# Experts written out instead of looped, router and last expert by halves, idle transposes in the opening: a two-layer encoder trunk on one core

## The chip, the cores and the metric

The kernel runs on 1 core of one Trainium2 chip, in float32 throughout. The metric is the device time of one execution in microseconds. Before the change three runs took 1687.43 to 1688.12 us, median 1687.98 us.

## The reference

Batch 1, 256 positions, width 1024, two layers. Both layers mix tokens in three branches; layer 0 ends with a dense SwiGLU, layer 1 with eight SwiGLU experts of which each token uses two. What matters here:

```python
for i in range(DEPTH):                                # 2 layers
    u = rmsnorm(h, norm_mix[i])
    z = u @ w_in[i]                                   # 1024 x 7620
    ...                                               # three token mixers
    h = h + merged @ w_out[i]
    v = rmsnorm(h, norm_ffn[i])
    if i % 2 == 0: h = h + swiglu(v, dense_wg[j], dense_wu[j], dense_wd[j])
    else:          h = h + moe_swiglu(v, moe_router[j], moe_wg[j], moe_wu[j], moe_wd[j])
    ple_g = sigmoid(rmsnorm(h, norm_ple[i]) @ ple_gate[i])
    h = h + ple_g * (p[i] @ ple_proj[i])
return rmsnorm(h, norm_final)

def moe_swiglu(v, router, wg, wu, wd):
    logits = v @ router
    top_val, top_idx = lax.top_k(logits, 2)
    top_w = softmax(top_val)
    combine = sum(one_hot(top_idx, 8) * top_w[..., None], axis=-2)
    for e in range(8):
        y = y + combine[..., e:e+1] * swiglu(v, wg[e], wu[e], wd[e])   # 1024 x 2816, 2816 x 1024
```

## The kernel before, in words

**Products in three parts.** Each weight is split into a high part (a copy by ScalarE into `whi`, `split_hi`) and a low part (the difference, by VectorE into `wlo`, `split_lo`); so are the activations (`ahi`, `alo`). A product of 128 x 128 by 128 x 512 is three TensorE matmuls (`three`, lines 1366 to 1368). Weights come in granules of 1 MB: two transfers issued by SP, into a ring of 4 slots (`RAW`), of 6 in the experts (`RAW_MOE`). A granule is converted 3 granules before its use (`WR`); SP refills a slot when the low part of its granule has been made (`split`, a wait on `lo_ready`). Each engine's program is written out in its order, and all meet by semaphores.

**Opening.** SP loads the first half of x and the first weights, ScalarE's queue the second half of x and the norm gains. GpSimd writes the identity. TensorE transposes the gains and, when x has landed, x (`transpose_h`, line 1426: 16 transposes of 128 x 128). ScalarE makes the high parts with the gain (line 557), VectorE the low parts (line 881), then both convert the first granules, and the first product starts.

**Router (layer 1).** When half 0 of h is there, TensorE transposes it; behind the last w_out granule, the other half. ScalarE and VectorE copy the transposes out with the gain (lines 716, 1199). 16 router products (line 1715, 32 instructions) follow when all is copied. VectorE finds the two largest logits, their weights, and from three (with the total five) small TensorE products the position of each token in its expert's list of 128 slots. `place_tokens` builds two selection matrices and two combine matrices (lines 1244, 1246). `gather` (lines 1733, 1734) multiplies v, in high and low part, by the selection: 16 instructions in each of two halves. `comb_transposed` turns the combine matrices (line 1739).

**Experts.** All five engines loop four times over two experts; counts of semaphores and the expert's number come from the loop's register. An expert has 33 granules (`ORDER`: two `up` granules for each of 11 slices of 256 channels, one `down` granule each); every granule is 12 matmuls of 512 columns. Behind `down` 2 and 4 stand the two combines of the *previous* expert (line 1747, four instructions each, then VectorE's add to h, line 1065), behind `down` 8 and 9 the gather for the *next* one. In the loop every expert has both: expert 0 combines a zeroed result `Y`, and expert 7 gathers for an expert 8 that selects nothing.

**Behind the experts.** TensorE turns p (line 1653), waits for its low part, does the two combines of expert 7 each followed by VectorE's add, takes a branch (`overflow`, into code for an expert with more than 128 tokens, not entered here), multiplies p by half 0 of ple_proj (12 matmuls), transposes h once VectorE's signal is there (the memset of line 1323, after its own branch), and does the gate products. At the end VectorE adds the gated part tile by tile, ScalarE squares (line 832), GpSimd takes the root (line 471), VectorE norms both tiles (line 866), and SP stores each.

## Time and profile before

| | before |
|---|---|
| median of three runs | 1687.98 us |
| profiled execution | 1688.75 us, of which 1687.0 us span |
| TensorE busy | 1632.1 us, 97% of the span |
| VectorE busy | 1288.3 us, 76% |
| ScalarE busy | 1016.6 us, 60% |
| GpSimd busy | 39.9 us, 2% |
| chain that ended last | 93% TensorE, 3% VectorE, 1% ScalarE, 1% transfers |
| transfers | 411.09 MB, mean 244 GB/s |

The profile shows one execution. The span runs from the first to the last instruction; the execution's own time is 1.75 us longer. A matmul overlaps the next one by its fill and drain, so the step from start to start counts, not the duration shown. Busy time says nothing of the clock: TensorE is as busy at 1.2 GHz as at 2.4 GHz, and "PEclk" in a window is the share of 2.4 GHz that was granted. In a row, "idle before" is how long the engine had stood still, and "<-" who released it.

### The profile page before, as it was taken

The page shows a single profiled execution, that of the slowest core. Times are in us where ns is not written, and L with a number is a line of the kernel's source. Part 1 is how long each engine was busy: PE and PEld are TensorE (multiplying, and loading weights), DVE is VectorE, ACT ScalarE, POOL GpSimd, SP SyncE. Part 2 cuts the span into 40 slices and gives each one's busy share as a digit, 9 for nine tenths or more (in the row PEclk, how much of TensorE's full clock was granted, in tenths as well). Part 3 has the DMA queues.
Part 4 walks back from the last instruction along what each step waited for, and adds up shares of the span by engine and source line. Part 5 has one row for each costly group of instructions (what it writes and reads, how often), then busy time and mean ns, then how long its engine had stood idle before and what let it go on. Part 6 is the DMA issues. An engine that isn't in the chain of part 4 may idle for free.

```text
span 1687.0 us, 22838 instructions
## 1 busy us (share of the span) xinstructions
PE 1632.1 (97%) x7729; PEld 1334.9 (79%) x7729; DVE 1288.3 (76%) x1528; ACT 1016.6 (60%) x1314; POOL 39.9 (2%) x70
## 2 busy tenths in 40 slices
PE   7999999999999999998999989999899998999987
PEld 6887888888888888887788777887788877888765
DVE  4786887545466886885798987989789897898974
ACT  4655434534455655333677776777777776777753
POOL 3100000000001000000000000000000000000000
PEclk9999999999999999997999999999999999999989
DMA  8444445555555454437799998999989999899950
GB/s 273 150 129 153 144 150 181 199 183 196 180 170 169 134 166 150 138 131 234 247 346 329 352 337 300 350 332 350 332 299 355 329 353 330 301 353 331 354 210 25
DMA packets 291217, 411.09 MB, mean 244 GB/s; under 512 B 15842, under 2 KB 221460, under 8 KB 291092
## 3 DMA queue, kind: packets, MB, share of 16 engines
q1 hardware_dynamic: 289296, 407.16, 71.7%
q10 hardware_dynamic: 1796, 2.32, 0.4%
q8 instruction: 71, 1.16, 0.3%
q14 instruction: 54, 0.44, 0.1%
HBM read 408.38 MB, written 1.05 MB: 243 GB/s over the span
## 4 chain that ended last, share of the span: by engine, by line
PE 93%; DVE 3%; issue 1%; DMA 1%; ACT 1%; POOL 0%; ACTq 0%; DVEq 0%; SPq 0%; POOLq 0%
PE ps L1366 27%; PE ps L1368 27%; PE ps L1367 27%; PE ps L1747 2%; PE ps L1591 1%; DVE wlo L849 1%; PE ps L1753 1%; PE ps L1464 1%; PE ps L1734 1%; PE ps L1733 1%; PE ps L1426 1%; PE ps L1474 1%; DMA arena<-in_moe_wu 1%; DVE arena L1122 0%; PE ps L1569 0%
## 5 line engine op out<-in xcount | busy, mean ns | idle before, releaser
L849 DVE TENSOR_TENSOR wlo<-arena,whi 128x1024 fp32r<-128x1024 f32 x774 | 910.9, 1219 | 177.4 <-ACT whi L516 166.2
L516 ACT ACTIVATE whi<-arena 128x1024 fp32r<-128x1024 f32 x774 | 774.1, 1052 | 173.8 <-PE ps L1368 163.9
L1366 PE MATMUL ps<-whi,ahi 128*128 128x512 f32 (+1 forms) x2040 | 824.7, 404 | 20.1 <-DVE wlo L849 18.5
L1368 PE MATMUL ps<-wlo,ahi 128*128 128x512 f32 (+1 forms) x2040 | 799.7, 392 | 0.0
L1367 PE MATMUL ps<-whi,alo 128*128 128x512 f32 (+1 forms) x2040 | 798.8, 392 | 0.0
L1366 PEld LDWEIGHTS ps<-whi,ahi 128*128 128x128 f32 x2040 | 386.0, 189 | 105.0 <-DVE wlo L849 18.7
L1368 PEld LDWEIGHTS ps<-wlo,ahi 128*128 128x128 f32 x2040 | 385.6, 189 | 82.9
L1367 PEld LDWEIGHTS ps<-whi,alo 128*128 128x128 f32 x2040 | 386.6, 190 | 78.5 <-issue 4.6
L849 DVE TENSOR_TENSOR alo<-ps,ahi 128x256 fp32r<-128x256 f32 (+3 forms) x137 | 71.3, 522 | 59.0 <-ACT ahi L516 40.5
L643 ACT ACTIVATE ahi<-ps 128x256 fp32r<-128x256 f32 x88 | 33.8, 384 | 109.4 <-PE ps L1753 109.2
L516 ACT ACTIVATE ahi<-ps 128x512 fp32r<-128x512 f32 (+2 forms) x49 | 29.3, 607 | 65.2 <-PE ps L1681 28.9
L516 ACT ACTIVATE arena<-ps 128x1024 f32<-128x1024 f32 (+2 forms) x41 | 32.7, 808 | 45.7 <-PE ps L1368 16.7
L787 ACT ACTIVATE arena<-ps 128x256 f32<-128x256 f32 x88 | 33.8, 384 | 40.6 <-PE ps L1368 40.6
L683 ACT ACTIVATE arena<-ps,small 128x512 f32<-128x512 f32 x24 | 15.2, 684 | 48.4 <-PE ps L1368 48.4
L1747 PE MATMUL ps<-arena 128*128 128x512 f32 x72 | 37.3, 644 | 5.9 <-DVE alo L849 4.6
L470 POOL TENSOR_SCALAR small<-small 128x2 f32<-128x2 f32 (+1 forms) x11 | 5.3, 485 | 1561.6 <-ACT arena L542 1206.2
L1065 DVE TENSOR_TENSOR h<-h,ps 128x1024 f32<-128x1024 f32 x24 | 29.1, 1213 | 13.2 <-PE ps L1747 7.5
L1279 DVE TENSOR_TENSOR arena<-arena,ps 128x256 f32<-128x256 f32 x88 | 36.4, 413 | 1.1 <-ACT arena L787 1.1
L1734 PE MATMUL ps<-ahi,alo 128*128 128x128 f32 x144 | 36.1, 291 | 0.0
L1733 PE MATMUL ps<-ahi 128*128 128x128 f32 x144 | 35.2, 284 | 0.0
L1753 PEld LDWEIGHTS ps<-ident,arena 128*128 128x128 f32 x176 | 23.9, 139 | 14.0 <-DVE arena L1279 3.6
L1753 PE MATMUL ps<-ident,arena 128*128 128x128 f32 x176 | 33.9, 274 | 0.3
(202 smaller groups left out, 812.8 us busy)
## 6 DMA issues: line engine op xcount, KB each, us to landing
arena<-in_moe_wg SPq DMA_DIRECT2D x176, 512.0 KB, 5.1
arena<-in_moe_wu SPq DMA_DIRECT2D x176, 512.0 KB, 6.7
arena<-in_moe_wd SPq DMA_DIRECT2D x176, 512.0 KB, 6.0
arena<-in_w_in SPq DMA_DIRECT2D x112, 512.0 KB, 4.5
arena<-in_w_branch SPq DMA_DIRECT2D x24, 512.0 KB, 4.6
arena<-in_dense_wg SPq DMA_DIRECT2D x22, 512.0 KB, 4.0
arena<-in_dense_wu SPq DMA_DIRECT2D x22, 512.0 KB, 5.0
arena<-in_dense_wd SPq DMA_DIRECT2D x22, 512.0 KB, 4.3
```

What stands on the lines that cost most here:

```text
L516: return nc.scalar.activation(dst, src, ACT.Copy)
L643: nc.scalar.activation(ahi[:, o:o + 256], bank(4, 256), ACT.Copy).then_inc(m_thi, 1)
L787: nc.scalar.activation(wk(SIL, FS), bank(s % 2, FS), ACT.Silu).then_inc(m_silu, 1)
L849: return V.tensor_tensor(dst, src, hi.bitcast(f32), ALU.subtract)
L1279: V.tensor_tensor(wk(FFN_, FS), wk(SIL, FS), bank(s % 2, FS, FS), ALU.mult)\
L1366: TE.matmul(o, ahi[:, sa], whi[:, sw], start=start, stop=False)
L1367: TE.matmul(o, alo[:, sa], whi[:, sw], start=False, stop=False)
L1368: return TE.matmul(o, ahi[:, sa], wlo[:, sw], start=False, stop=stop)
L1733: TE.matmul(o, ahi[:, vc:vc + P], psel[:, t * P:(t + 1) * P], start=t == 0, stop=False)
L1734: last = TE.matmul(o, alo[:, vc:vc + P], psel[:, t * P:(t + 1) * P], start=False, stop=t == 1)
L1747: last = TE.matmul(bank(6 + half), wk(CSB + q * 256 + t * P, P), wk(Y + half * 512, 512), start=True, stop=True)
L1753: last = TE.transpose(bank(4, P, c * P), wk(FFN_ + c * P, P), ident[:, :])
```

## The change

- *Opening.* SP loads both halves of x ahead of the weights; ScalarE's queue starts with the gains. ScalarE makes one small copy as soon as the identity is there, ahead of its wait for the gains. TensorE runs 16 transposes of the identity before it waits for the gains, and 24 more behind the transposes of x, into a bank that is not read.
- *Router.* The router products are issued by chunks of the width: 0 to 3 behind the last w_out granule, 4 and 5, then 6 and 7, behind the transposes of half 1. ScalarE squares tile 0 of h before it copies chunks 4 and 5 out, and tile 1 after. The total per expert (for the overflow test) goes to a bank and semaphore of its own, and VectorE reads it behind the first conversions of expert 0. The positions are copied in one instruction; the two selection matrices come before the two combine matrices; the gather stands before the transposes of the combine matrices and waits for the first two alone. `up` granule 0 of an expert waits for half 0 of its tokens, granule 1 for half 1.
- *Experts.* All engines have 8 x 33 granules written out, with constants. Expert 0 has no combines and expert 7 no gather. In expert 7, p is turned and split behind `down` 6, where other experts turn the next combine matrices.
- *Last expert.* Its last granule is multiplied by output half; each half is copied out, combined for both tiles and added to h by half. The high and low part of p lie in another place.
- *Final norm.* VectorE multiplies h by the final gain per half, beside the last squares; then VectorE scales tile 0 and ScalarE tile 1 by the root, and each store waits for its tile.

```diff
@@ SP: x, and the experts' weights
-            sp.dma_start(h[:, 0:D], x[0, 0:P, :]).then_inc(x_landed, 16)
+            for t in range(NT):
+                sp.dma_start(h[:, t * D:(t + 1) * D], x[0, t * P:(t + 1) * P, :]).then_inc(x_landed, 16)
...
-            with sp.Fori(0, NE // 2) as it:
-                for m in range(2 * PER_E):
-                    split(M0 + m - RAW_MOE, it)
-                    e = it * 2 + m // PER_E
+            for m in range(N_MOE):
+                split(M0 + m - RAW_MOE)
+                e = m // PER_E
...
@@ ScalarE: opening, router, last copy of an expert, end
-            act.dma_start(h[:, D:2 * D], x[0, P:2 * P, :]).then_inc(x_landed, 16)
...
+                    act.wait_ge(pool_consts, 2)
+                    copy(lbt[:, 12:13], ident[:, 0:1])
                     act.wait_ge(gains_ready, 1)
...
+                    act.wait_ge(h_half, h_ready(1, "out", 1))
+                    square_of(0)
                     for c in range(4, 6):
                         vt_out(c)
-                norm_squares(h_half, h_ready(layer, "out", 1))
+                    square_of(1)
...
+                            if k == PER_E - 1:
+                                act.wait_ge(combined, 2 * e)
+                                if e < NE - 1:
+                                    act.wait_ge(gemm_done, n + 1)
                                     copy(wk(Y, 1024), bank(2, 1024)).then_inc(m_y, 1)
+                                else:
+                                    for half in range(2):
+                                        act.wait_ge(*((down_half, 2) if half == 0 else (gemm_done, n + 1)))
+                                        copy(wk(Y + half * 512, 512), bank(2 + half)).then_inc(m_y, 1)
+                            convert(n + WR)
...
+            act.wait_ge(rstd_ready, 3 * DEPTH + 1)
+            act.wait_ge(u_ready, 4)
+            nc.scalar.activation(u_nat(1), u_nat(1), ACT.Copy, scale=rstd(3 * DEPTH, 1)).then_inc(out_scaled[1], 1)
@@ VectorE: router, last adds, end
-                    V.memset(wk(Y, 1024), 0.0).then_inc(m_y, 1)
...
-                    for t in range(NT):
-                        V.tensor_copy(wk(POS + 16 * t, 8), bank(1, 8, 8 * t))
-                    link(V.reduce_max(wk(GAP + 48, 1), bank(1, 8, 16), AX.X))
-                    V.tensor_copy(biggest[:, :], wk(GAP + 48, 1)).then_inc(pos_ready, 1)
-                    dve.wait_ge(pos_ready, 1)
+                    link(V.tensor_copy(by_tile(POS, 8, 16), bank(1, 16).rearrange("p (t k) -> p t k", k=8)))
...
-                    lo_of_p()
-                    for t in range(NT):
-                        add_combined(t, 2 * NE + t + 1)
-                        dve.wait_ge(comb_added, 2 * NE + t + 1)
+                    for half in range(2):
+                        dve.wait_ge(last_combined, half + 1)
+                        add_to_h(h_half_of(half), bank(6 if half == 0 else 0, 1024).rearrange("p (t f) -> p t f", t=NT))\
+                            .then_inc(comb_added, 1)
+                    dve.wait_ge(comb_added, 2 * NE)
...
+                        dve.wait_ge(gain_row_landed, 32)
+                        dve.wait_ge(h_last, 2 * half + 2)
+                        for t in range(NT):
+                            o = slice(half * 512, half * 512 + 512)
+                            V.tensor_tensor(u_nat(t)[:, o], h[:, t * D + half * 512:t * D + half * 512 + 512], gain_row[:, o],
+                                            ALU.mult).then_inc(u_ready, 1)
...
-            norm(3 * DEPTH, 2)
+            dve.wait_ge(rstd_ready, 3 * DEPTH + 1)
+            V.tensor_scalar(u_nat(0), u_nat(0), rstd(3 * DEPTH, 0), None, ALU.mult).then_inc(out_scaled[0], 1)
@@ TensorE: opening
+            def keep_busy(n):
+                for _ in range(n):
+                    last = TE.transpose(bank(5, P), ident[:, :], ident[:, :])
+                return last
+
             pe.wait_ge(pool_consts, 2)
+            keep_busy(16)
             pe.wait_ge(gains_landed, 64)
...
             for half in range(2):
                 transpose_h("mix", half)
+            keep_busy(24)
@@ TensorE: router and gather
+                    pe.wait_ge(vt_act, 4)
+                    router_products(range(4))
                     pe.wait_ge(h_half, h_ready(1, "out", 1))
                     transpose_h("moe", 1)
                     pe.wait_ge(vt_act, 6)
+                    router_products(range(4, 6))
                     pe.wait_ge(vt_dve, 2)
+                    router_products(range(6, 8)).then_inc(router_done, 1)
...
                     pe.wait_ge(v_lo, NT)
+                    for half in range(2):
+                        gather(half, onehot, 2, gathered)
                     pe.wait_ge(onehot, 4)
                     comb_transposed()
@@ TensorE: experts
+                    for e in range(NE):
+                        q = e % 2
+                        for k, (kind, j, part) in enumerate(ORDER):
+                            n, s = M0 + e * PER_E + k, e * NS + j
+                            if kind == "up":
+                                if k < 2:
+                                    pe.wait_ge(xg_hi, 2 * e + k + 1)
+                                    pe.wait_ge(xg_lo, 2 * e + k + 1)
...
+                            if k == PER_E - 1 and e == NE - 1:
+                                for half, done in ((0, down_half), (1, gemm_done)):
+                                    by_half(n, n % WR, FFT + 256 * (s % 2), half, [bank(2 + half)], False, True, P)\
+                                        .then_inc(done, 1)
...
+                            if j in (2, 4) and e > 0:
...
+                                combine(1 - q, t)
+                            if j == 6:
...
+                                else:
+                                    pe.wait_ge(ct_out, NE)
+                                    turn_p()
+                            if j in (8, 9) and e + 1 < NE:
...
+                                gather(j - 8, onehot, 4 * e + 8, gathered)
+                    pe.wait_ge(comb_added, 2 * NE - 2)
+                    for half in range(2):
+                        pe.wait_ge(m_y, NE + half)
+                        for t in range(NT):
+                            last = TE.matmul(bank((6 if half == 0 else 0) + t), wk(CSB + q * 256 + t * P, P),
+                                             wk(Y + half * 512, 512), start=True, stop=True)
+                        last.then_inc(last_combined, 1)
```

## Rows read from the trace of the kernel before

**Rows 1.** TensorE's waits over the whole span: us in total, times, longest.

```profile
PE ps L1366 <- DVE wlo L849: 18.5, 4, 5.3
```

**Rows 2.** Timeline of the opening: start us, us, engine, line, instruction, [idle before <-releaser].

```profile
7.97 3.44 PE L1426 MATMUL ps<-ident,h 128*128 128x128 f32 x16
...
9.17 1.28 ACT L557 ACT_TABLE_LOAD   x1 [9.17 <-PE ps L1426]
...
14.38 0.71 PE L1366 MATMUL ps<-whi,ahi 128*128 128x512 f32 x1 [2.97 <-DVE wlo L849]
```

**Rows 3.** The chain that ended last: start us, us, what.

```profile
477.44 1.75 PE ps L1426 x16
...
837.62 1.72 PE ps L1747 x4
```

**Rows 4.** Windows in the opening: us, busy by engine, PEclk, DMA share, GB/s.

```profile
14.00:14.50 0.50, 0.12 (x1) 0.15 (x2) 0.50 (x2) 0.50 (x1) 0.00 (x0) 0.94 1.03 377
14.50:15.00 0.50, 0.50 (x2) 0.41 (x3) 0.50 (x1) 0.50 (x2) 0.00 (x0) 0.50 1.08 393
```

**Rows 5.** Timeline of the router passage.

```profile
779.65 1.09 PE L1426 MATMUL ps<-ident,h 128*128 128x128 f32 x8 [1.86 <-DVE h L1065]
...
781.81 6.40 PE L1715 MATMUL ps<-router,arena 128*128 128x8 f32 x32 [1.07 <-ACT arena L716]
...
790.68 2.48 DVE L1231 SCALAR_TENSOR_TENSOR alo<-arena,small,ahi 128x1024 fp32r<-128x1024 f32 x2
...
795.18 0.46 PE L1733 MATMUL ps<-ahi 128*128 128x128 f32 x1
...
803.85 0.79 PE L1366 MATMUL ps<-whi,ahi 128*128 128x512 f32 x1 [1.60 <-DVE alo L849]
```

**Rows 6.** Windows from a combine to the next, across the three boundaries, and their sum.

```profile
938.16:1046.27 108.11, 102.94 (x461) 83.10 (x461) 89.67 (x97) 76.98 (x94) 0.00 (x0) 0.97 0.95 324
...
sum 324.02, PE 308.38 PEld 249.01 DVE 269.07 ACT 230.94 POOL 0.00; mean PE 102.79 PEld 83.00 DVE 89.69 ACT 76.98 POOL 0.00
```

**Rows 7.** The same, the four that lie inside a pass.

```profile
837.62:938.16 100.54, 100.52 (x462) 81.34 (x461) 89.60 (x97) 74.29 (x92) 0.00 (x0) 1.00 1.00 341
...
sum 401.62, PE 401.49 PEld 325.37 DVE 358.42 ACT 297.20 POOL 0.00; mean PE 100.37 PEld 81.34 DVE 89.61 ACT 74.30 POOL 0.00
```

**Rows 8.** Timeline from the last expert to the transposes of h.

```profile
1632.64 0.60 PE L1653 MATMUL ps<-ident,arena 128*128 128x128 f32 x4
...
1637.86 3.78 PE L1747 MATMUL ps<-arena 128*128 128x512 f32 x4 [4.62 <-DVE alo L849]
...
1642.95 3.49 PE L1747 MATMUL ps<-arena 128*128 128x512 f32 x4 [1.31 <-DVE h L1065]
...
1649.00 0.06 DVE L1323 MEMSET arena<- 128x1 f32 x1 [1.23 <-issue]
...
1649.11 1.97 PE L1426 MATMUL ps<-ident,h 128*128 128x128 f32 x16
```

**Rows 9.** Timeline of the end.

```profile
1681.33 2.48 DVE L866 SCALAR_TENSOR_TENSOR arena<-h,small,arena 128x1024 f32<-128x1024 f32 x2 [2.17 <-POOL small L471]
1682.64 1.55 SPq L425 DMA_DIRECT2D out_h<-arena  x2
```

**Rows 10.** Timeline of half a gather: its first product and the first behind it.

```profile
902.64 0.22 PE L1733 MATMUL ps<-ahi 128*128 128x128 f32 x1
...
904.37 0.44 PE L1366 MATMUL ps<-whi,ahi 128*128 128x512 f32 x1
```

**Rows 11.** Groups by shape: scaling by a value per row on VectorE.

```profile
L910 DVE TENSOR_SCALAR arena<-arena,small 128x256 f32<-128x256 f32 x2 | 0.7, 354 | 4.7 <-ACT arena L612 4.7
...
L910 DVE TENSOR_SCALAR arena<-arena,small 128x128 f32<-128x128 f32 x2 | 0.6, 288 | 0.6 <-ACT arena L610 0.5
```

**Rows 12.** Windows of 10 us inside the first pass of the expert loop.

```profile
830.00:840.00 10.00, 10.00 (x43) 7.56 (x42) 9.91 (x15) 7.80 (x10) 0.00 (x0) 1.00 1.06 363
...
980.00:990.00 10.00, 10.00 (x47) 8.24 (x46) 9.33 (x10) 7.69 (x10) 0.00 (x0) 1.00 0.75 279
```

More of the change, by code:

```diff
@@ L311, in build @@
         XG, FFT = 2048, 4096
+        PT = (4096, XG)
         def blocks(ap, m):
@@ L859, in convert @@
                     split_lo(n % WR, raw_of(n), width_of(n), lambda i: dve.wait_ge(hi_ready, 2 * n + i + 1))
-            def norm(r, done):
-                dve.wait_ge(rstd_ready, r + 1)
-                dve.wait_ge(gain_row_landed, 16 * done)
-                for t in range(NT):
-                    V.scalar_tensor_tensor(out=u_nat(t), in0=h[:, t * D:(t + 1) * D], scalar=rstd(r, t),
-                                           in1=gain_row, op0=ALU.mult, op1=ALU.mult).then_inc(u_ready, 1)
             split = [0]
@@ L1401, in wide_granule, with by_half @@
                 ins.then_inc(gemm_done, 1)
-            def by_half(n, ring, a_base, half, outs, first, last):
+            def by_half(n, ring, a_base, half, outs, first, last, a_pitch=SEQ):
                 for c in range(2):
@@ L1407, in by_half @@
                     for t, o in enumerate(outs):
-                        ins = three(o, a_base + c * SEQ + t * P, ring * GRAN + c * D + half * 512, 512,
+                        ins = three(o, a_base + c * a_pitch + t * P, ring * GRAN + c * D + half * 512, 512,
                                     first and c == 0, last and c == 1)
@@ L1707, in _, with router_products @@
                 else:
+                    pe.wait_ge(router_landed, 16)
+                    def router_products(chunks):
+                        for c in chunks:
+                            for t in range(NT):
+                                last = TE.matmul(bank(2 + t, NE), wk(VT + c * SEQ + t * P, P),
+                                                 router[:, c * NE:(c + 1) * NE], start=c == 0, stop=c == KC - 1)
+                        return last
+                    pe.wait_ge(vt_act, 4)
+                    router_products(range(4))
                     pe.wait_ge(h_half, h_ready(1, "out", 1))
@@ L1710, in _ @@
                     pe.wait_ge(vt_act, 6)
+                    router_products(range(4, 6))
                     pe.wait_ge(vt_dve, 2)
-                    pe.wait_ge(router_landed, 16)
-                    for t in range(NT):
-                        for c in range(KC):
-                            last = TE.matmul(bank(2 + t, NE), wk(VT + c * SEQ + t * P, P),
-                                             router[:, c * NE:(c + 1) * NE], start=c == 0, stop=c == KC - 1)
-                    last.then_inc(router_done, 1)
+                    router_products(range(6, 8)).then_inc(router_done, 1)
                     pe.wait_ge(sel_ready, 1)
@@ L1721, in _ @@
                     TE.matmul(bank(1, NE, 8), ones[:, :], s0, start=True, stop=False)
[L1722 to L1724 removed]
+                    TE.matmul(bank(1, NE, 8), later[:, :], s1, start=False, stop=True).then_inc(pos_done, 1)
+                    TE.matmul(bank(4, NE), ones[:, :], s0, start=True, stop=False)
+                    TE.matmul(bank(4, NE), ones[:, :], s1, start=False, stop=True).then_inc(total_done, 1)
                     def gather(half, ready, onehot_value, done):
@@ L1850, in _ @@
                 pe.wait_ge(pt_lo, layer + 1)
-                by_half(first, first % WR, 4096, 0, [bank(PROJ[0] + t) for t in range(NT)], True, True)
+                by_half(first, first % WR, PT[layer], 0, [bank(PROJ[0] + t) for t in range(NT)], True, True)
                 for half in range(2):
@@ L1854, in _ @@
                     transpose_h("ple", half)
-                by_half(first, first % WR, 4096, 1, [bank(PROJ[1] + t) for t in range(NT)], True, True).then_inc(gemm_done, 1)
+                by_half(first, first % WR, PT[layer], 1, [bank(PROJ[1] + t) for t in range(NT)], True, True).then_inc(gemm_done, 1)
                 for i, (half, q) in enumerate(PLE_ORDER[1:]):
```

225 lines of the change are left out of this document (100 added, 125 removed).

## The prediction

> **What bounds the kernel now.** I read first the share of busy time: TensorE 97%. The chain of waits that ended last is 93% TensorE, so a change pays where TensorE stands still, works at its lower clock, or does work that nobody needs. The list of waits names the first kind [rows 1]: 18.5 us before products that wait for VectorE's low parts, in four waits: the opening and three loop boundaries. The timeline of the opening shows 16 transposes over 3.44 us, 215 ns each [rows 2]; 16 of them take 1.75 us at the full clock [rows 3]. So the opening ones ran at 1.2 GHz. The clock record first drops to half at 14.4 us [rows 4]; a clock that drops had been full, so it rose behind those transposes and was lost in the 3 us of idleness before the first product at 14.38. The router passage is a chain of small steps with TensorE at half clock [rows 5]. The experts are a loop of four passes with two experts each; cut at the same combine product in every expert, the time from one to the next is 108.0 us across a boundary [rows 6] and 100.4 us inside a pass [rows 7]. The last stretch is serial again: combines, adds and transposes one after the other [rows 8], then root, norm and stores [rows 9].
>
> **The sum, part by part** (against the profiled execution, 1687.0 us of span, 1688.75 us in all; the median of the runs shown is 0.77 us below that).
>
> *Opening.* SP takes the second half of x, the gains start one issue (0.4 us) sooner, ScalarE loads its table before it is needed, and TensorE runs 16 idle transposes before the gains and 24 behind the transposes of x. The table load stands in the chain now: 1.28 us between the transposes and the first high part [rows 2]. With it gone and the gains sooner the first low weights are ready at 14.38 - 1.28 - 0.45 = 12.6 us, at most 0.3 us sooner still. TensorE starts no earlier than the 24 transposes allow: x's transposes end near 11.0; if the clock rises there, as it did before, 24 x 0.109 = 2.6 us put the first product at 13.6. That is 0.8 us, and the eight products that ran 427 ns apart instead of 227 give 1.7 (the cold stretch was 14.38 to 17.87). Together 2.5; I take 2.6 as the 16 earlier ones may raise the clock already (then 3.8). If the idle transposes do not hold the clock, 24 x 0.215 = 5.2 us end at 16.2 and the opening loses 1.8. Bounds -1.8 and 3.8; the drop at 14.4 is the row nearest to this case, and it speaks for holding.
> The Trainium skill (ScalarE: Activation LUTs, What ACT_TABLE_LOAD costs) gives a switch of tables 1283 ns and a drain of some 1380 ns more. The trace has the first, and the next instruction 20 ns behind it, so the drain isn't there; by the page the low weights would be ready 1.4 us earlier still, which the 24 transposes would swallow.
>
> *Router.* Four of the eight pairs of router products move into TensorE's wait for the second half of h. Before, all 32 instructions took 6.40 us from 781.81 at mostly half clock [rows 5]. Now 16 run in the gap from 777.6 (ending near 779.4), 8 behind the fifth and sixth chunk, 8 behind VectorE's two. ScalarE squares tile 0 before those chunks, which puts them at 781.8 instead of 781.2, and its second square ends a little sooner. Router end: 781.85 + 0.8 + 1.6 = 784.3 instead of 788.2. VectorE's chain is the same 2.4 us up to the low parts of v, about 0.3 us longer since the two sigmoids now queue behind ScalarE's high parts: low parts from 787.05, 2.48 us, then one copy and two selections (0.75) instead of two copies, a maximum, a cast and four selections: gather at 790.35, against 795.18. After the gather TensorE waited 1.6 us for the high and low part of the second half; now expert 0 asks only for the first half, which was ready during the second gather, and the two combine transposes (0.45) stand there instead: 1.2 more. Sum 6.0, with the gathers and the first products still at half clock. Bounds 4.0 and 9.5 (clock full, below). The moved maximum and the four later operations on VectorE lie beside the products of expert 0.
>
> *Expert 0's empty combine.* Before, expert 0 added a zeroed result: two combines of 1.72 us each [rows 3]; 3.5 with the slower product behind them. VectorE's two adds and two memsets go with them, hidden.
>
> *Loop boundaries.* The three intervals with a boundary make 324.02 us [rows 6], the four without 401.62 [rows 7], 100.4 each: 324.0 - 3 x 100.4 = 22.8 us. Each is some 5.1 us of idleness (the register and branch work of ScalarE, VectorE and TensorE one after the other, then low parts) and then 12 products at 427 instead of 227 ns. Written out, the step from expert 1 to 2 is the step from 0 to 1, which shows no wait. Bounds 21 and 23.5: inside a pass an expert is 0.7 us longer than its products, transposes, combines and gathers add up to, so there is little more in constants instead of registers.
>
> *Last expert.* The gather for an expert that doesn't exist goes: two halves of 1.73 us [rows 10]; four transposes of p come where two combine transposes were (+0.3). 3.2.
>
> *From the experts to the gate.* T is the end of the last expert's products, 1632.64 now [rows 8]. Today p is turned behind T, its high and low parts queue behind conversions, and the two combines start at 1637.86, at half clock, each followed by VectorE's add: 3.78 and 3.49 us. The transposes of h start at 1649.11 = T + 16.5. In the new order half 0 of the result is complete 1.4 us before T and ScalarE copies it (0.6) before T; the four combine products run from T at full clock (2 x 1.72 = 3.44), the add of half 0 beside half 1. Then TensorE does the first 12 products of p (2.72): T + 6.2. VectorE: T + 3.5, add 1.22, 1.23 us of branch work before its signal (as the idle time before the memset shows): T + 6.05. So the transposes start at T + 6.2: 10.3 us. If TensorE's own branch shows, 1.2 less; bounds 8.5 and 10.6. What is late next is the branch on VectorE, level with the products of p.
>
> *The end.* The last norm was 2 x 1.24 us on VectorE behind the root, the stores behind each [rows 9]. Now the gain is multiplied in by VectorE while the last square and the root run (2 x 0.69 from 1679.2, done before 1681.25), and the two tiles are scaled side by side: ScalarE 1.05, VectorE from its rows of 128 and 256 elements, 288 and 354 ns [rows 11], an estimated 288 + 7 x 66 = 750 ns. The second store can go at 1682.5 instead of 1683.8, but the two transfers then overlap more. I take 0.9, bounds 0.3 and 1.3.
>
> Sum: 2.6 + 6.0 + 3.5 + 22.8 + 3.2 + 10.3 + 0.9 = 49.3 us. 1688.75 - 49.3 = 1639.45 for the profiled execution, 0.77 less for the median: 1638.7 us.
>
> **Rivals.** (a) *The stream of weights becomes the bound.* The experts read 528 transfers of 524,288 bytes, 276.8 MB, now in 829 us from their first product; without the boundaries, the combine and the gather it is 799 us, 346 GB/s. For: the transfer share stands near 1.0 in most windows, and a boundary is a rest for the stream. Against: ScalarE never waits for a transfer inside the experts, windows reach 363 GB/s, and late in a pass (980 to 990) the stream idles a quarter of the time because the ring is full [rows 12]. If some 333 GB/s were the most, experts would take as long as before and 29.5 us would be lost: 1668 us. Chance 0.05. The Trainium skill (DMA: Bandwidth & Descriptors, the table of limits at its head) gives about 358 GB/s of HBM per core; by that, as an estimate, the experts need 773 us at least, under my 799, but expert 0 alone (97 us, 357 GB/s) stands at the edge, and would be the place where it first shows.
> (b) *Only the expert part pays.* The idle transposes run at half clock and delay the opening by 1.8, the router chain gives 3 as another small step is late, the tail gives 6 and the stores nothing: 29.5 - 1.8 + 3 + 6 = 36.7, 1651 us. For: these parts hang on semaphores in a row, where one overlooked step takes a microsecond each. Against: each term above is half removed work. Chance 0.08.
> (c) *The clock stays full through the router*, as TensorE now has work where it idled from 777.6 to 779.6: 32 gather products 0.104 us shorter and 12 to 14 of the first expert products 0.2 us shorter give 6 us more, 1632.6 us. Against: the 6.4 us of router products, busy throughout, did not hold it before. Chance 0.08.
> (d) *Slower than before*: the written-out instructions of four engines come late, because they share the transfer engines with weights at 350 GB/s. It decides from 49.3 us over the 264 granules of the experts, 0.19 us per granule; at 0.25 it would be 1704 us. Against: one pass is already 200 us without a jump, and TensorE shows no such wait there. Chance 0.02.
>
> **How the numbers follow.** Forecast 0.77, (a) 0.05, (b) 0.08, (c) 0.08, (d) 0.02. The lower bounds of all terms add up to 38.3 us (1649.7), the upper ones to 55.9 (1632.1); all at one end is unlikely, so 1632 to 1647 holds the forecast and (c), and most of what lies short of (b). 0.2% is 3.4 us, about what a measurement of this kernel can tell from no change: faster 0.97, same 0.01, slower 0.02.
>
> **What would show it.** The intervals between the same combine product in successive experts: all near 100.4 us, the first shorter by 3.5, none of 108. First product near 13.6 us, 227 ns to the next. Gather near 795.2 - 2.6 - 4.8 = 787.8 and expert 0 from 795.3. h transposed 6.2 us behind the last expert product. Wrong would be: ScalarE waiting for transfers inside the experts (a), the idle transposes 215 ns apart to their end (b), gathers 109 ns apart (c), or new waits on no semaphore in the experts (d).

## The result and the profile after

The changed kernel takes 1640.55 us (median of four runs, 1639.43 to 1640.70), the kernel before in the same comparison 1687.70 us (1686.59 to 1688.12): ratio 0.972, 95% interval 0.9703 to 0.9737. The forecast was 1638.7 us. Profiled against profiled it is 1688.75 to 1640.61 us, 48.1 us less, where the sum had 49.3. Below, each stretch is read at one instruction that both kernels have; the column "earlier" is how much sooner it starts, counted from the start of the span, and "this stretch" is what the stretch itself gave.

| at | before | after | earlier | this stretch | forecast |
|---|---|---|---|---|---|
| end of the opening, ninth product of 512 columns | 17.87 | 15.07 | 2.80 | 2.8 | 2.6 |
| expert 0, transposes behind slice 1 | 814.89 | 804.94 | 9.95 | 7.2 | 6.0 |
| expert 0, its slice 9 | 900.97 | 887.29 | 13.68 | 3.7 | 3.5 |
| first instruction behind the last expert's products (T) | 1632.64 | 1593.29 | 39.35 | 23.4 loops, 2.3 last expert | 22.8, 3.2 |
| transposes of h behind the experts | 1649.11 | 1601.04 | 48.07 | 8.7 | 10.3 |
| end of the span | 1687.0 | 1638.9 | 48.1 | 0.0 | 0.9 |

The page of the changed kernel: shares of busy time, and the transfers in 40 slices (GB/s).

```profile
PE 1615.3 (99%) x7727; PEld 1327.3 (81%) x7727; DVE 1284.1 (78%) x1520; ACT 1007.3 (61%) x1307; POOL 38.8 (2%) x70
...
GB/s 284 152 129 154 155 129 188 194 195 181 190 187 179 132 145 149 144 145 190 226 365 351 363 352 335 350 333 362 352 335 351 328 364 345 339 354 330 353 291 26
```

Full slices of the experts now move 328 to 365 GB/s, and ScalarE waits for no transfer there: rival (a) is refuted. Four slices lie above the 358 GB/s of that rival's estimate (365, 363, 362 and 364). TensorE's list of waits, changed kernel (us in total, times, longest), answers to [rows 1]; of the 18.5 us none is left:

```profile
PE ps L1744 <- DVE arena L1227: 2.1, 1, 2.1
PE ps L1435 <- DVE arena L1328: 1.4, 1, 1.4
PE ps L1757 <- DVE ahi L1245: 1.4, 1, 1.4
...
PE ps L1378 <- issue: 1.0, 1, 1.0
```

The first row is the router's small products, which waited 2.1 us before the change too; the third is the router's wait for the selection matrices. The second and the fourth are new: 1.4 us before the transposes of h and 1.0 before a product of the last expert.

*Opening*, timeline of the changed kernel, for [rows 2]:

```profile
2.15 3.67 PE L1624 MATMUL ps<-ident 128*128 128x128 f32 x16 [2.15 <-POOL ident L444]
...
2.78 1.28 ACT L517 ACT_TABLE_LOAD   x1 [2.78 <-issue]
...
7.19 3.57 PE L1435 MATMUL ps<-ident,h 128*128 128x128 f32 x16
...
10.60 2.79 PE L1624 MATMUL ps<-ident 128*128 128x128 f32 x24
...
13.13 0.48 PE L1378 MATMUL ps<-whi,ahi 128*128 128x512 f32 x1
...
13.45 0.40 PE L1379 MATMUL ps<-whi,alo 128*128 128x512 f32 x1
```

The 24 transposes take 2.79 us, the full clock, and the product behind is followed after 0.32 and then 0.24 us. Half clock would put 0.43 between them.

*Router*, the same timeline, for [rows 5]:

```profile
774.87 1.84 PE L1730 MATMUL ps<-router,arena 128*128 128x8 f32 x16
...
778.25 3.37 PE L1730 MATMUL ps<-router,arena 128*128 128x8 f32 x16 [0.61 <-ACT arena L721]
...
784.10 2.48 DVE L1236 SCALAR_TENSOR_TENSOR alo<-arena,small,ahi 128x1024 fp32r<-128x1024 f32 x2
...
787.46 0.44 PE L1757 MATMUL ps<-ahi 128*128 128x128 f32 x1 [1.41 <-DVE ahi L1245]
...
794.31 0.65 PE L1763 MATMUL ps<-ident,arena 128*128 128x128 f32 x2
```

The first 16 router instructions take 1.84 us, 115 ns each, at the full clock. The second 16 start behind 0.61 us of idleness and take 3.37: the granted clock falls from 1.00 to 0.50 at 778.5, 0.3 us into them. The gather runs at half clock.

*Experts*, windows from a combine to the next, for [rows 6, 7]: no interval is longer than another.

```profile
924.34:1024.65 100.31, 100.27 (x462) 81.43 (x461) 89.64 (x97) 74.29 (x92) 0.00 (x0) 1.00 1.01 346
...
1425.82:1526.08 100.26, 100.22 (x462) 81.43 (x461) 89.14 (x94) 74.29 (x92) 0.00 (x0) 1.00 1.01 347
sum 601.74, PE 601.52 PEld 488.58 DVE 537.37 ACT 445.75 POOL 0.00; mean PE 100.25 PEld 81.43 DVE 89.56 ACT 74.29 POOL 0.00
```

*Last expert to the transposes of h*, timeline, for [rows 8]:

```profile
1587.69 2.36 DVE L863 TENSOR_TENSOR wlo<-arena,whi 128x1024 fp32r<-128x1024 f32 x2
...
1588.50 0.38 ACT L647 ACTIVATE ahi<-ps 128x256 fp32r<-128x256 f32 x1
...
1589.97 0.42 DVE L863 TENSOR_TENSOR alo<-ps,ahi 128x256 fp32r<-128x256 f32 x1
1590.49 0.47 PE L1378 MATMUL ps<-whi,ahi 128*128 128x512 f32 x1 [0.97 <-issue]
...
1593.29 3.59 PE L1841 MATMUL ps<-arena 128*128 128x512 f32 x8
...
1593.98 2.00 ACT L517 ACTIVATE whi<-arena 128x1024 fp32r<-128x1024 f32 x2
1595.06 2.36 DVE L863 TENSOR_TENSOR wlo<-arena,whi 128x1024 fp32r<-128x1024 f32 x2 [1.99 <-ACT whi L517]
1597.34 2.35 DVE L1071 TENSOR_TENSOR h<-h,ps 128x1024 f32<-128x1024 f32 x2
1600.93 0.06 DVE L1328 MEMSET arena<- 128x1 f32 x1 [1.24 <-issue]
1601.04 1.97 PE L1435 MATMUL ps<-ident,h 128*128 128x128 f32 x16 [1.43 <-DVE arena L1328]
```

VectorE's queue is the story, twice. The high part of the last slice's transposes is ready at 1588.88, but VectorE is in a conversion until 1590.05, makes the low part by 1590.39, and the product starts 0.10 us behind it (1590.49). The profile names no releaser for that stall of 0.97 us; the product starts 0.10 us behind the same low part in three kernels below, too. Then VectorE waits 1.99 us for a high part, makes a low part that nobody needs yet (2.36), and then comes to the two adds (2.35), its branch (1.24) and the signal.

*End*, timeline, for [rows 9]:

```profile
1631.20 1.29 DVE L1363 TENSOR_TENSOR arena<-h,arena 128x512 f32<-128x512 f32 x2
...
1631.93 0.62 POOL L479 TENSOR_TENSOR small<-small 128x2 f32<-128x2 f32 x1 [24.03 <-ACT arena L843]
...
1633.65 1.15 ACT L848 ACTIVATE arena<-arena,small 128x1024 f32<-128x1024 f32 x1 [1.79 <-POOL small L472]
1633.72 0.75 DVE L1367 TENSOR_SCALAR arena<-arena,small 128x1024 f32<-128x1024 f32 x1 [1.22 <-POOL small L472]
1634.50 0.83 SPq L426 DMA_DIRECT2D out_h<-arena  x2
```

### The profile page after: what moved, and what is told of

Its sections match the earlier page's. It is cut to its first block, busy times and chain, and to the rows that moved or that the text cites. A ratio compares the mean times of both kernels' runs of the same rounds, so it can differ in the third digit from the quotient of the medians.

```text
span 1638.9 us, 20095 instructions
## 1 busy us (share of the span) xinstructions
PE 1615.3 (99%) x7727; PEld 1327.3 (81%) x7727; DVE 1284.1 (78%) x1520; ACT 1007.3 (61%) x1307; POOL 38.8 (2%) x70
## 4 chain that ended last, share of the span: by engine, by line
PE 95%; DVE 3%; issue 1%; ACT 0%; DMA 0%; POOL 0%; ACTq 0%; POOLq 0%; DVEq 0%
PE ps L1378 28%; PE ps L1380 28%; PE ps L1379 27%; PE ps L1600 2%; PE ps L1771 1%; PE ps L1777 1%; PE ps L1473 1%; PE ps L1758 1%; PE ps L1435 1%; PE ps L1757 1%; DVE wlo L863 1%; PE ps L1483 1%; DVE arena L1128 0%; PE ps L1578 0%; DVE arena L1123 0%
## 5 line engine op out<-in xcount | busy, mean ns | idle before, releaser
L679 ACT ACTIVATE arena<-ps,small 128x512 f32<-128x512 f32 (+1 forms) x16 | 10.9, 682 | 37.8 <-PE ps L1380 37.8
L1757 PE MATMUL ps<-ahi 128*128 128x128 f32 x128 | 31.7, 286 | 1.4 <-DVE ahi L1245 1.4
L1758 PE MATMUL ps<-ahi,alo 128*128 128x128 f32 x128 | 32.4, 293 | 0.0
L1186 DVE SCALAR_TENSOR_TENSOR arena<-ps,small,arena 128x256 f32<-128x256 f32 x22 | 9.6, 480 | 28.4 <-ACT arena L751 28.4
```

Of the source, the lines that this page charges most:

```text
L1757: TE.matmul(o, ahi[:, vc:vc + P], psel[:, t * P:(t + 1) * P], start=t == 0, stop=False)
L1758: last = TE.matmul(o, alo[:, vc:vc + P], psel[:, t * P:(t + 1) * P], start=False, stop=t == 1)
```

## The experiments

Kernels that ran together share a chip and its runs of the kernel before: medians 1686.7 us for the loop experiments, 1686.65 for the next four, 1686.57 for the last four. The medians of the kernel before differ by up to 1.4 us from comparison to comparison and its single executions by up to 9 (1682.2 to 1691.3), so ratios are compared, and where they can't decide, rows.

### Loops: which engine's jump costs what

All four change the kernel before. First, every loop of the experts is written out, with nothing else of the change:

```diff
-                    with <engine>.Fori(0, NE // 2) as it:
+                    for it in range(NE // 2):
```

> The kernel before with nothing changed but the expert loops of all engines, written out (empty combine and empty gather stay). Both theories: the three boundaries and only they go, 3 x 7.6 to 7.8 = 23 us (1664.7 us), all intervals between combines near 100.3 us. If the written-out code cost something elsewhere (instructions that come late), less than 20 us.

1662.77 us (1662.30 to 1662.99), ratio 0.9862 (0.9846 to 0.9879): 24 us less. The window across its first boundary is like one of the changed kernel:

```profile
936.88:1037.22 100.34, 100.30 (x462) 81.44 (x461) 89.63 (x97) 74.30 (x92) 0.00 (x0) 1.00 1.01 345
```

So the loops alone are worth 24 us, half of the change, and the other parts together the other half. Next, the same edit in TensorE's program only:

> Only TensorE's expert loop is written out; SP, ScalarE and VectorE still loop. Theory A (TensorE's own jump is the 5.1 us; the others run three granules ahead and hide theirs): nearly all of the 23 us go, 1665 to 1668 us. Theory B (the prediction's: the jumps of ScalarE, VectorE and TensorE one after the other, then low parts): TensorE still waits at each boundary, 3 x 2 us and more remain, 1671 us or above.

1676.79 us (1672.72 to 1680.17), ratio 0.9936 (0.9918 to 0.9954): 10 us less. The three intervals with a boundary fall from 108.0 us to between 104.26 and 104.62, not to 100.3. Its waits of TensorE, and a timeline of its first boundary:

```profile
PE ps L1753 <- DVE arena L1279: 7.1, 3, 2.7
```

```profile
1012.41 1.28 ACT L516 ACT_TABLE_LOAD   x1
1015.73 1.28 ACT L787 ACT_TABLE_LOAD   x1
1017.57 2.36 DVE L849 TENSOR_TENSOR wlo<-arena,whi 128x1024 fp32r<-128x1024 f32 x2 [3.73 <-issue]
...
1020.31 0.69 PE L1753 MATMUL ps<-ident,arena 128*128 128x128 f32 x2 [2.72 <-DVE arena L1279]
```

TensorE runs on into the next expert and meets VectorE, which lost 3.73 us in its own jump; ScalarE's loop has two table loads in each pass, eight in all; with ScalarE written out there is one in the whole expert part. Then the reverse, SP, ScalarE and VectorE written out and TensorE in its loop:

> The reverse: SP, ScalarE and VectorE written out, TensorE still loops. Theory A: no gain, 1686 to 1688 us, intervals of 108 us stay. Theory B: one to three us per boundary go, 1679 to 1685 us.

1682.31 us (1678.00 to 1684.81), ratio 0.9973 (0.9961 to 0.9985): 4.4 us less, the intervals 104.73, 106.99 and 107.79. TensorE's jump alone costs 4.4 to 7.5 us per boundary with its slow products. Its idleness there is 2.56, 3.71 and 4.54 us; why it differs from boundary to boundary is open. 10 and 4.4 do not add up to 24: each jump hides part of the other's. Either time alone lies where the prediction's serial account put it; the two together contradict it. Removing one jump uncovers the other, which is why the prediction, which priced the boundary as a whole, came out and a price per engine would not have. Last, TensorE in its loop is given work to the very end of each pass:

```diff
+                        pe.wait_ge(ct_out, it * 2 + 3)
+                        for _ in range(32):
+                            TE.transpose(bank(5, P), ident[:, :], ident[:, :])
```

> The kernel before with 32 transposes of the identity at the end of each of the four passes of TensorE's loop, 3.5 us of work at full clock in the 5.1 us of idleness. If the second part of a boundary's price is the clock, the 12 products behind it run 227 instead of 427 ns apart and an interval falls from 108.0 to 105.6 us, 3 x 2.4 = 7 us in all (1680.5 us), the last pass adding up to 1 us. If the jump waits until the transposes are done, the idleness comes behind them and the interval grows by up to 3.5 us instead.

1693.91 us, ratio 1.0046 (1.003 to 1.0062): 7 us slower, intervals 111.1 us. Timeline of its first boundary:

```profile
1006.54 3.65 PE L1806 MATMUL ps<-ident 128*128 128x128 f32 x32
1014.80 0.79 PE L1366 MATMUL ps<-whi,ahi 128*128 128x512 f32 x1 [4.61 <-issue]
1015.39 0.63 PE L1367 MATMUL ps<-whi,alo 128*128 128x512 f32 x1
```

The 4.61 us stand behind the transposes, released by nothing that the profile shows (4.62 and 4.52 at the other two boundaries, against 5.09 to 5.30 without the transposes). So 3.65 us of filler hide 0.5 to 0.8 us: the jump hardly runs beside work that is still queued, and the clock is lost in it all the same: 0.59 and 0.43 us from product to product.

### Opening: what holds the clock

The experiments from here on change the changed kernel. Both groups of idle transposes go:

```diff
-            keep_busy(16)
...
-            keep_busy(24)
```

> The changed kernel without the 16 and the 24 idle transposes of the opening; the early table load and the order of loads stay. If the clock is what the idle transposes buy: first product at 12.3 us instead of 13.1, but the first 8 to 12 products 427 ns apart; the opening is 0.8 us quicker to its first product and 1.7 to 2.5 us slower after it, in all about 1.3 us slower than the changed kernel (1641.9 us). If they bought nothing, 0.9 us faster.

1639.09 us (1638.13 to 1640.43), ratio 0.972 (0.9703 to 0.9737), the ratio of the changed kernel. The half clock isn't there: the first product starts sooner than in the changed kernel, and at full clock.

```profile
7.17 3.52 PE L1435 MATMUL ps<-ident,h 128*128 128x128 f32 x16
12.37 0.47 PE L1378 MATMUL ps<-whi,ahi 128*128 128x512 f32 x1 [1.68 <-DVE wlo L863]
12.68 0.39 PE L1379 MATMUL ps<-whi,alo 128*128 128x512 f32 x1
```

Left are 1.68 us of idleness instead of the 2.97 before [rows 2]. Is it the shorter idleness, then? The next kernel also gives up the early table load, so that the idleness grows back:

```diff
-                    act.wait_ge(pool_consts, 2)
-                    copy(lbt[:, 12:13], ident[:, 0:1])
```

> The changed kernel without the idle transposes and without the early one-column copy, so that ScalarE loads its table (1.28 us) behind the first transposes of x again. Without the idle transposes alone the gap behind the last of the 16 transposes of x was 1.7 us and the first product (12.37) ran at full clock. Theory (the gap's length decides): the gap grows to 3.0 us as in the kernel before, the first product comes at 13.65 and the clock is at half for some products behind it, as it was before; time +1.3 for the load and +0.9 to 1.5 for the clock: 1641.3 to 1641.9 us, ratio 0.9732. Rival (the clock was held by something else, such as the earlier transposes of the norm weights at 6.9): the clock stays full, +1.3 only: 1640.4, ratio 0.9726. The granted clock in the windows behind the first product tells them apart, whatever the time.

1641.01 us, ratio 0.9731 (0.9716 to 0.9746). Timeline, then a window (the last three numbers are PEclk, DMA share, GB/s):

```profile
8.44 1.28 ACT L561 ACT_TABLE_LOAD   x1 [8.44 <-PE ps L1433]
...
13.66 0.47 PE L1376 MATMUL ps<-whi,ahi 128*128 128x512 f32 x1 [2.74 <-DVE wlo L861]
```

```profile
14.50:15.00 0.50, 0.50 (x3) 0.40 (x2) 0.50 (x2) 0.50 (x2) 0.00 (x0) 0.50 1.05 385
```

First product 1.29 us later, and the clock lost behind it, as the theory said. Later profiles (their kernels follow) showed that neither kernel's opening runs the same way each time:

| kernel | idle transposes | 16 transposes of x | first product | clock behind it |
|---|---|---|---|---|
| changed | yes | 3.57 us | 13.13 | full |
| router products together | yes | 3.26 us | 12.94 | full |
| p later | yes | 1.97 us | 11.74 | full |
| later convert | yes | 1.97 us | 11.85 | full |
| no idle transposes | no | 3.52 us | 12.37 | full |
| gain behind the root | no | 3.52 us | 12.60 | full |
| three edits | no | 3.38 us | 12.53 | half from 13.8 |
| table late | no | 3.67 us | 13.66 | half from 14.4 |

In two of four profiles the 16 early transposes brought the full clock to the transposes of x, the case that the forecast kept as its upper bound. Without any, the clock fell in one of three profiles with the early table load, behind 1.82 us of idleness against 1.68 and 1.67 in the others. That one reached the router 1.5 us later than its neighbour (779.19 against 777.70, the second group of router products), and 0.8 us of it came back there, as is said below. So the idle transposes cost up to 0.8 us in some executions and give 0.7 us in others, or 0.9 to 2.2 where the clock would have been lost. With them the first product comes at 12.4 us in the mean of four profiles; without, at 13.0 in the mean of three, if the lost clock's 1.5 us is counted in. That leans to keeping them and settles nothing. The openings differ by up to 1.4 us within one of these groups, where the times of one kernel's runs differ by 1.3 to 3.3.

### Router: products in chunks or together

All 32 router instructions stand behind the last copies again, and ScalarE's first square behind its two copies (that part of the edit is not shown):

```diff
-                    pe.wait_ge(vt_act, 4)
-                    router_products(range(4))
...
-                    router_products(range(4, 6))
...
-                    router_products(range(6, 8)).then_inc(router_done, 1)
+                    router_products(range(8)).then_inc(router_done, 1)
```

> The changed kernel with the router products in one go behind the last copy, and ScalarE's squares behind its copies, as before. Router products then end 3.5 to 4 us later (32 instructions at half clock, 6.4 us), and the total is 3.5 us higher, 1644 us. If the clock does not drop sooner or later for it, the first expert products cost the same. Rival: the chain behind the router absorbs it (GpSimd's root or ScalarE's high parts are what VectorE waits for): under 1.5 us.

1643.38 us, ratio 0.9741 (0.9724 to 0.9758), 2.8 to 3.5 us over the changed kernel (its time, its ratio). Waits of TensorE that the changed kernel has shorter or not at all:

```profile
PE ps L1435 <- DVE h L1071: 1.4, 1, 1.4
```

The prediction had 3.9 us for this step (788.2 to 784.3). In the rows the gather comes 3.7 us later (791.15), or 3.9 counted from each kernel's first product, so the chain behind the router absorbs nothing. The edit undoes the chunks and the order of the squares together; which gives what is not shown.

The same router code, too, runs in more than one way. This is the second group of products in the kernel "p later", below:

```profile
776.81 1.95 PE L1730 MATMUL ps<-router,arena 128*128 128x8 f32 x16 [0.61 <-ACT arena L721]
```

It takes 1.95 us, the full clock, in four of the seven kernels compared here, 2.76 in two and 3.37 in the changed kernel, each time behind 0.61 us of idleness; where the clock held, it fell in the wait behind the group. The gather ran at half clock in all of them. From the start of this group to the transposes behind slice 1 of expert 0 it is 26.69 us in the changed kernel and 25.07 to 25.96 in the six others: its profile is the slowest of the seven in this passage.

### The last stretch

VectorE's conversion of the third granule of the ple weights moves behind the signal that h is complete:

```diff
-                            convert(n + WR)
+                            if k < PER_E - 1 or e < NE - 1:
+                                convert(n + WR)
...
                     V.memset(wk(GAP, 1), 0.0).then_inc(h_half, 2)
+                    convert(M0 + N_MOE - 1 + WR)
```

> The changed kernel with VectorE's conversion of the third ple granule moved from ahead of the two last adds to behind its signal to TensorE. Theory: this conversion (2.36 us, waiting for ScalarE) is what stands between the last combines and the transposes of h; the adds start at 1595.2 and 1597 instead of 1597.3, the transposes of h start 6.1 to 6.3 us behind the last expert product instead of 7.6, total 1.4 us less (1639.1). Rival: the branch of VectorE or the products of p are late by themselves, and less than 0.5 us goes.

1637.73 us (1637.27 to 1639.25), ratio 0.9712 (0.9697 to 0.9726). Its timeline:

```profile
1591.51 3.59 PE L1843 MATMUL ps<-arena 128*128 128x512 f32 x8
...
1593.42 1.22 DVE L1071 TENSOR_TENSOR h<-h,ps 128x1024 f32<-128x1024 f32 x1 [2.16 <-PE ps L1843]
...
1597.71 1.97 PE L1437 MATMUL ps<-ident,h 128*128 128x128 f32 x16
```

From the combines to the transposes of h it is 6.20 us, against 7.75: 1.55 us, and TensorE's wait for VectorE's signal is gone. The profiles differ by more than that in places that the edit doesn't touch: 1.28 us in the opening and 1.39 in the router (its small products start at 781.07, against 783.74). Next, p is turned behind `down` 9 instead of `down` 6, here in VectorE's program and likewise in TensorE's and ScalarE's:

```diff
-                            if kind == "down" and j == 6 and e == NE - 1:
+                            if kind == "down" and j == 9 and e == NE - 1:
```

> The changed kernel with p turned behind the tenth w_down product of the last expert instead of the seventh, nothing else. If the 0.97 us stall before the last granule is only for want of work between the ff transposes and it, it shrinks to about 0.4 and the time is 1640.0 us, ratio 0.9717. Rival: VectorE's low part of p (0.42 us) now stands in its queue ahead of the low part of ff, so the stall stays 0.97 or grows by 0.4: 1640.5 to 1641.

1638.90 us (1636.91 to 1640.17), ratio 0.9717 (0.9702 to 0.9732). The stall before the last granule shrinks from 0.97 to 0.53 us:

```profile
1587.62 0.47 PE L1378 MATMUL ps<-whi,ahi 128*128 128x512 f32 x1 [0.53 <-issue]
```

By its median alone this would be unclear; the row shows it, 0.44 us for some 0.5 us of work put there. The stall is want of cover for that low part, and the rival is out: p's low part came at 1590.12, behind it in VectorE's queue. A conversion stands ahead of the low part that is waited for (1584.82, 2.36 us, here too); to put the low part first was not tried. The three edits together (no idle transposes, late convert, p later):

> Three edits to the changed kernel together: no idle transposes; VectorE's convert of the third granule of the ple weights behind the last expert's h signal; gates p of the last layer turned (and its high part copied) behind the tenth w_down product instead of the seventh. If the 0.97 us wait before the last granule is the low part of the ff transposes having lost the gather that covered it, p's turn of some 0.5 us put there fills part of it: -0.4 to -1. With the -0.8 of the idle transposes and -2.8 of the later convert: 1636.1 us (1635.3 to 1637.5), ratio to the kernel before 0.9700. Rival (the savings overlap, since each ends in a wait on the same VectorE queue): 1637.7, no better than the later convert alone.

1636.66 us (1635.91 to 1638.58), ratio 0.9704 (0.9691 to 0.9717), by its median the fastest kernel here, at 0.9704 against 0.972 with intervals that overlap; the late convert alone has 0.9712, so the times do not tell whether the other two edits add to it. Its rows have both gains of the last stretch, 0.54 us of stall and 6.21 from combines to transposes. The last kernel adds to these three a wait of VectorE for the root before it multiplies the second half by the gain:

```diff
+                        if half == 1:
+                            dve.wait_ge(rstd_ready, 3 * DEPTH + 1)
```

> The first kernel of this call (three edits) with one more: VectorE waits for the root of the final norm before it multiplies the second half's two tiles by the gain row. Theory (GpSimd's root is slowed from 0.19 to 0.62 us by VectorE's two-input operations beside it): GpSimd's first operation takes 0.2 us again and the root is ready 0.4 us earlier, but VectorE's two products then start behind it; what ends the span is the pair of stores, so the net is a loss of 1 us or so (the products take 1.29 for two, of which all is now behind the root, against 0.4 gained): +0.9 us against the first kernel. Rival (GpSimd's 0.62 is the first operation's own, whatever stands beside it): the operation still takes 0.62 and the loss is +1.3.

1638.28 us (1637.40 to 1639.02), ratio 0.9714 (0.9699 to 0.9729). Its timeline:

```profile
1627.79 0.20 POOL L479 TENSOR_TENSOR small<-small 128x2 f32<-128x2 f32 x1 [24.03 <-ACT arena L843]
...
1629.18 1.29 DVE L1367 TENSOR_TENSOR arena<-h,arena 128x512 f32<-128x512 f32 x2 [2.22 <-POOL small L472]
...
1631.29 0.83 SPq L426 DMA_DIRECT2D out_h<-arena  x2
```

GpSimd's first operation takes 0.20 us again: it was the two VectorE multiplications beside it that made it 0.62. From ScalarE's last accumulator read (1627.53) to the first store it is 3.76 us, against 2.83 with the overlap (1629.67 to 1632.50, three edits): 0.93 us lost, 0.9 expected. The overlap pays, although it makes GpSimd 0.42 us slower. The same edit alone on the changed kernel was run before:

> The changed kernel with VectorE's multiplication of half 1 by the final gain moved behind GpSimd's root. Theory: GpSimd's first operation took 0.62 instead of 0.19 us because VectorE ran a two-input operation beside it; alone it takes 0.19 again and the root is ready 0.43 us sooner, while the two multiplications (1.29 us) now stand behind it: 0.9 us slower in all. Rival: GpSimd's operation stays at 0.6 us, and the total is 1.3 us slower.

Of its two runs the profiled one took 2696.0 us at a mean granted clock of 0.561, the other 1638.66 us: too little for a comparison. GpSimd's first operation took 0.20 us in that profile too.

## Why the prediction was right, and where it was not

The total is closer than its parts. The stretches miss by -1.6, -0.9 and -0.9 us where something else was late next, and by +1.2, +0.2, +0.2 and +0.6 elsewhere: 3.4 us too little and 2.2 too much. That they cancel to 1.2 is luck. The bounds given for the terms, with 3.5 and 3.2 for the two that have none, add up to 38.7 and 55.4 us, not to 38.3 and 55.9.

*Loops, 22.8 us: right* (23.4; 24 by the experiment that wrote out loops alone). The constants made an expert 0.1 us shorter, of 0.7 at most. The mechanism as worded, register and branch work of three engines one after the other, was too simple: the jumps run in part beside one another (10 and 4.4 us singly, 24 together), and all but 0.5 to 0.8 us of TensorE's idleness stands behind whatever work is put ahead of it.

*Expert 0's empty combine, 3.5 us: right* (3.7).

*Router, 6.0 us: mis-sized by 1.2* (7.2). The steps came as said: counted without the opening's 2.76 us the gather was expected 4.8 us earlier and came 4.96 earlier, at 787.46. The order behind it gave 1.5 instead of 1.2, and then the full clock came back after 10 slow products instead of 13 or 14, 0.7 us that the sum had not. This term depends on the execution: by the six other profiles of the passage it would be 0.7 to 1.6 us more. Gather and first products ran at half clock in all of them, so (c) is refuted: 16 busy instructions in the gap held the clock through the second group in four profiles, and in none up to the gather.

*Opening, 2.6 us: the size right* (2.8), *the working half right*. The first product at 13.13, 0.5 before the forecast's 13.6, because the 24 transposes started at 10.60, not 11.0. That they hold the clock is not needed as a cause: where low weights come 1.3 us sooner the clock mostly holds without them, and the upper case of x's transposes at full clock, left aside, is as frequent. The Trainium skill (ScalarE: Activation LUTs, What ACT_TABLE_LOAD costs) counts a drain of some 1380 ns with a load. Here it isn't seen: the early load at 2.78 ends at 4.06 and the next instruction starts at 4.08, and the load at 1015.73 in "Loops" stands between an instruction that ends at 1015.71 and one that starts at 1017.02. Taking the load out of the chain gave 1.1 to 1.3 us (first product at 12.37 to 12.60 in three profiles, against 13.66), about its own 1.28, and not 2.7.

*Last expert, 3.2 us: mis-sized* (2.3). The removed gather had been the cover of the low part of the last slice's transposes: 1.73 us of gather, and under them 0.42 us of VectorE. With it gone TensorE stands for 0.97 us, as a conversion of 2.36 us is ahead of that low part in VectorE's queue. The step said what goes and what comes, and not who was late underneath.

*From the experts to the gate, 10.3 us: mis-sized by 1.6* (8.7). The transposes start at T + 7.75 instead of T + 6.2. The products were where they should be; "VectorE: T + 3.5, add 1.22" failed. It placed the adds by their inputs and forgot the queue ahead of them, in which a conversion waits for ScalarE and then takes 2.36 us. Putting it behind the signal gave T + 6.20 (1591.51 to 1597.71), the forecast.

*The end, 0.9 us: wrong* (0.0). VectorE's scaling took exactly the estimated 0.75 us and the second store was issued 0.4 instead of 1.2 us behind the first. The term counted from the second store's issue, and that failed: from the first store's issue to the end it is 4.4 us before and after (1682.64 to 1687.0, 1634.50 to 1638.9), whenever the second is issued. "The two transfers then overlap more" had named this without a price. And the first store came no sooner, because GpSimd's root was 0.43 us later by the multiplications beside it, which took back most of the 0.5 us that the shorter scaling gave.

Rivals (a) to (d) did not occur; no engine waited for instructions in the written-out experts (instruction queues moved 62 and 34 packets, fewer than the loops' 71 and 54).

## What to carry to other kernels

Price a loop boundary as a whole, from interval against interval, and remove it on all engines: one engine's jump hides another's, so halves of the edit gave 10 and 4.4 us where the whole gave 24. Where work is removed, ask which other engine's result was being made beneath it; where an instruction's inputs come sooner, read the queue ahead of it on its engine. Two misses here, 1.6 and 0.9 us, are these two questions not asked, and both times the answer was a conversion of 2.36 us in VectorE's queue.

## What the runs showed of the hardware that was not expected

- TensorE's idleness at its jump back: 5.09 to 5.30 us with all engines looping, 4.52 to 4.62 behind 32 transposes (3.65 us of work), 2.56, 3.71 and 4.54 when TensorE alone loops.
- With ScalarE in its loop every pass has two table loads (2 x 1.28 us, eight loads in all); written out, the expert part has one.
- A GpSimd operation on 128 x 2 elements takes 0.62 us beside VectorE's two-input operation on 128 x 512, and 0.19 to 0.20 without it.
- In the opening TensorE's clock survived 1.67 and 1.68 us of idleness and fell behind 1.82, 2.74 and 2.97 us. These are five executions; all have the same 17 TensorE instructions ahead of the idleness. In the router, with 0.61 us of idleness each time, it fell within the next 16 instructions in three profiles and held through them in four. The length of the idleness alone does not decide.
- The same opening runs in two ways: the 16 transposes of x took 1.97 us in two profiles and 3.26 and 3.57 in two others, with the first product at 11.74 and 11.85 or at 12.94 and 13.13.
